# The gate row ahead of the last two experts' scatter, and a later start for GpSimd

## What is computed

```python
for e in range(N_EXPERTS):
    hid = jax.nn.silu(t @ w1[e]) * (t @ w3[e])
    out = out + gate[:, e:e + 1] * (hid @ w2[e])
...
x = x + g_f[:, None] * _hier_moe(hf, ...)
```

## Time and profile before

| | us |
|---|---|
| median of 3 runs | 1541.68 |
| lowest, highest | 1541.16, 1543.71 |
| profiled execution, its own time | 1542.04 |
| its span, first to last instruction | 1540.2 |
| TensorE busy | 1512.9 (98%) |
| VectorE busy | 1186.7 (77%) |
| ScalarE busy | 948.8 (62%) |
| GpSimd busy | 80.1 (5%) |

### The profile page before, as it was taken

The page is one execution under the profiler, slowest core; times in us unless marked ns, Lnnn a source line. Parts: engine busy times, 40 slices in busy tenths (PEclk is TensorE's granted clock), DMA queues, the critical chain, the costliest instruction groups (busy, mean ns, idle before and its releaser), DMA issues.

```text
span 1540.2 us, 20164 instructions
## 1 busy us (share of the span) xinstructions
PE 1512.9 (98%) x7920; PEld 1257.1 (82%) x7920; DVE 1186.7 (77%) x1639; ACT 948.8 (62%) x1503; POOL 80.1 (5%) x78
## 2 busy tenths in 40 slices
PE   9999999999999999999999999999999899999997
PEld 9998888888888799888788887887777778888785
DVE  7568857667888684788576679877667789999998
ACT  6577854755444364878457555544455568888884
POOL 0010000000000000100000000000200000000005
PEclk9999999999999999999999999999999999999999
DMA  7545436437776445453455368884521449999994
GB/s 293 209 142 205 149 137 218 148 127 277 254 269 242 161 177 187 159 191 136 164 191 192 137 244 326 333 321 142 192 103 55 159 188 366 367 380 372 374 365 163
DMA packets 52200, 339.33 MB, mean 220 GB/s; under 512 B 7835, under 2 KB 8477, under 8 KB 13316
## 3 DMA queue, kind: packets, MB, share of 16 engines
q1 hardware_dynamic: 48932, 331.79, 58.3%
q0 software_dynamic: 3168, 6.20, 1.1%
HBM read 332.82 MB, written 10.49 MB: 223 GB/s over the span
## 4 chain that ended last, share of the span: by engine, by line
PE 47%; DVE 6%; ACT 2%; issue 1%; DMA 0%; POOL 0%; DVEq 0%; ACTq 0%
PE bank L842 14%; PE bank L844 13%; PE bank L843 13%; PE bank L848 3%; DVE wls L2285 2%; PE bank L1380 1%; DVE h L2255 1%; ACT whs L1603 1%; PE bank L1362 1%; PE bank L1182 0%; PE bank L1160 0%; DMA raw<-in_ws_dram 0%; PE bank L1099 0%; POOL sm L3256 0%; PE bank L1122 0%
## 5 line engine op out<-in xcount | busy, mean ns | idle before, releaser
L2285 DVE TENSOR_TENSOR wls<-raw,whs 128x1024 fp32r<-128x1024 f32 x432 | 514.1, 1226 | 149.0 <-ACT whs L1603 148.1
L1603 ACT ACTIVATE whs<-raw 128x1024 fp32r<-128x1024 f32 x432 | 435.9, 1052 | 189.1 <-PE bank L844 164.2
L842 PE MATMUL bank<-whs,P1h 128*128 128x512 f32 (+1 forms) x732 | 291.3, 398 | 2.0 <-issue 2.0
L844 PE MATMUL bank<-whs,P1l 128*128 128x512 f32 (+1 forms) x732 | 285.0, 389 | 0.0
L843 PE MATMUL bank<-wls,P1h 128*128 128x512 f32 (+1 forms) x732 | 284.1, 388 | 0.0
L842 PE MATMUL bank<-whs,P0h 128*128 128x512 f32 (+1 forms) x632 | 251.6, 398 | 1.4 <-DVE P0l L2255 1.4
L844 PE MATMUL bank<-whs,P0l 128*128 128x512 f32 (+1 forms) x632 | 245.1, 388 | 0.0
L843 PE MATMUL bank<-wls,P0h 128*128 128x512 f32 (+1 forms) x632 | 244.5, 387 | 0.0
L842 PEld LDWEIGHTS bank<-whs,P1h 128*128 128x128 f32 x732 | 138.0, 188 | 29.9 <-issue 3.4
L844 PEld LDWEIGHTS bank<-whs,P1l 128*128 128x128 f32 x732 | 137.9, 188 | 29.6
L843 PEld LDWEIGHTS bank<-wls,P1h 128*128 128x128 f32 x732 | 138.2, 189 | 26.7
(11 more groups left out here) (298 smaller groups left out, 2521.9 us busy)
## 6 DMA issues: line engine op xcount, KB each, us to landing
raw<-in_ws_dram SPq DMA_DIRECT2D x264, 1024.0 KB, 4.8
landing<-in_ws_dram SPq DMA_DIRECT2D x38, 1024.0 KB, 7.2
lnb<-in_ln_g_dram SPq DMA_DIRECT2D x6, 512.0 KB, 6.1
lnb<-in_ln_b_dram SPq DMA_DIRECT2D x6, 512.0 KB, 7.2
ydram<-arena POOLq DMA_DIRECT2D x4, 512.0 KB, 8.4
mid<-in_bias_dram SPq DMA_DIRECT2D x1, 2048.0 KB, 7.5
h<-in_x_dram SPq DMA_DIRECT2D x2, 512.0 KB, 4.0
lnb<-in_mem_dram SPq DMA_DIRECT2D x1, 1024.0 KB, 12.4
```

The lines of the kernel that those rows point to most:

```text
L842: e.matmul(out, x[0], w[0], start=start, stop=False, skip_group_check=skip)
L844: return e.matmul(out, x[1], w[0], start=False, stop=stop, skip_group_check=skip)
L1603: e.activation(hi, src, ACT.Copy, bias=0.0, scale=1.0).then_inc(*high.done(n, f))
L2285: e.tensor_tensor(lo, src, f32(hi), ALU.subtract).then_inc(*low.done(n, f))
```

## The change

Four things are done, all in the last stage:

- For experts 14 and 15 VectorE multiplies each bank by the gate row into `Y` (new key `yg`), ScalarE copies `Y`, not the bank, to `Yph`, and VectorE subtracts from `Y`, not from the bank. Both products stand ahead of both subtractions. The scatter's result then needs no product, so that VectorE adds the banks to `h` directly, in four additions.
- The order of these additions and of the stores is by column half first, and all four are VectorE's; GpSimd's two last additions are gone.
- GpSimd's product of fetched rows and gate row waits, besides the combination, for the last weight half (`low` of the last unit).
- VectorE's combination for t = 1 (`combined(1)`) moves from chunk 31's `combine` to behind the subtraction of `turn_hidden(31)`. On ScalarE `combine` stays where it is.

```diff
@@ TensorE, down_part and scatter
-                                bank(b, (act if x < NFAR else vec, "ey", x, hf))
+                                bank(b, (act, "ey", x, hf) if x < NFAR else (vec, "yg", x, hf))
...
-                                bank(b, (vec, "fin", t, hf))
+                                bank(b, (vec, "out", t, hf))
@@ ScalarE, down_part
-                        ac.wait_ge(mm, "edn", c, hf)
-                        wait_for(start)
                         if x < NFAR:
+                            ac.wait_ge(mm, "edn", c, hf)
+                            wait_for(start)
...
                         else:
+                            ac.wait_ge(vec, "yg", x, hf)
                             if x > NFAR:
                                 ac.wait_ge(mm, "eacc", x - 1, 1, 1)
-                            put(Yp[0][:, o], banks[b][:, :], ACT.Copy, "ey", x, hf)
+                            put(Yp[0][:, o], Y[x % 2][:, o], ACT.Copy, "ey", x, hf)
@@ VectorE, turn_hidden
                     tt(hid[1][:, s_], halves(banks[7][:, 0:256]), f32(hid[0][:, s_]), ALU.subtract, "ehT", c)
+                    if c == 2 * NEXP - 1:
+                        combined(1)
@@ VectorE, down_part
                     for hf in range(2):
                         b = ((6, 4) if x == NEXP - 1 else (3, 6) if x % 2 else (2, 1))[hf]
                         o = slice(hf * 512, (hf + 1) * 512)
+                        ve.wait_ge(mm, "edn", c, hf)
+                        ve.wait_ge(sent[x % 2], x - 2)
+                        ve.wait_ge(vec, "rows", 3)
+                        tt(Y[x % 2][:, o], banks[b][:, :], gab[:, 1, o], ALU.mult, "yg", x, hf)
+                    for hf in range(2):
+                        o = slice(hf * 512, (hf + 1) * 512)
                         ve.wait_ge(act, "ey", x, hf)
-                        tt(Yp[1][:, o], banks[b][:, :], f32(Yp[0][:, o]), ALU.subtract, "ey", x, hf)
+                        tt(Yp[1][:, o], Y[x % 2][:, o], f32(Yp[0][:, o]), ALU.subtract, "ey", x, hf)
@@ VectorE, combine
                 def combine(t):
+                    if t == 0:
+                        combined(t)
+
+                def combined(t):
                     a, b = far[t], far[2 + t]
@@ VectorE, the end
-                for t in range(2):
-                    for n in range(2):
-                        s_, o = slice(n * 512, (n + 1) * 512), arr(512 * (2 * n + t), 512)
+                for n in range(2):
+                    for t in range(2):
+                        s_ = slice(n * 512, (n + 1) * 512)
                         ve.wait_ge(mm, "eacc", NEXP - 1, t, n)
-                        tt(o, banks[2 * n + t][:, :], gab[:, 1, s_], ALU.mult, "fin", t, n)
-                        if n:
-                            ve.wait_ge(vec, "fin", t, n)
-                            ve.wait_ge(pool, "h", t)
-                            tt(h[:, t, s_], h[:, t, s_], o, ALU.add, "out", t, n)
+                        ve.wait_ge(pool, "h", t)
+                        tt(h[:, t, s_], h[:, t, s_], banks[2 * n + t][:, :], ALU.add, "out", t, n)
@@ GpSimd
                     po.wait_ge(vec, "comb", t)
+                    po.wait_ge(low, len(plan) - 1, 1)
                     po.wait_ge(vec, "rows", 3)
...
-                for t in range(2):
-                    po.wait_ge(vec, "fin", t, 0)
-                    po.wait_ge(pool, "h", t)
-                    e.tensor_tensor(h[:, t, 0:512], h[:, t, 0:512], arr(512 * t, 512), ALU.add).then_inc(*pool.done("out", t, 0))
@@ SyncE, stores
-            def stores(key):
-                for t in range(2):
-                    for n in range(2):
-                        sp.wait_ge((pool, vec)[n], key, t, n)
+            def stores(key, by):
+                for n in range(2):
+                    for t in range(2):
+                        sp.wait_ge(by[n], key, t, n)
...
-                stores("out")
+                stores("out", (vec, vec))
```

More of the change, by code:

```diff
@@ L3436, in sparse @@
                 weights(list(paths[1]))
-                stores("out")
+                stores("out", (vec, vec))
             def dense():
                 weights(list(paths[0]))
-                stores("dout")
+                stores("dout", (pool, vec))
             two_ways(sp, None, sparse, dense)
```

## The result

| | before | changed |
|---|---|---|
| median of 14 runs, us | 1540.93 | 1543.88 |
| lowest, highest | 1539.91, 1544.25 | 1542.51, 1545.60 |
| profiled execution: time, span | 1542.04, 1540.2 | 1544.08, 1542.3 |
| VectorE's end, from z | 16.06 | 17.37 |
| end of the span, from z | 19.70 | 22.77 |

The ratio of the changed kernel's time to the one before is 1.0017, 95% interval 1.0010 to 1.0025: the changed kernel is slower, by 2.95 us between the medians. The forecast was 1542.1 with a range up to 1543.3, so the time lies above the range.

The account below looks back on a forecast made before the run. VectorE rows held behind GpSimd's instructions were taken to delay down chunk 31. The 1.4 us gained there was eaten by GpSimd's late sum, leaving plus 0.43 on the median 1541.68: 1542.1 us, range 1540.2 to 1543.3.

Parts of the forecast that it names:

- The waiting and its release: Ahead of down chunk 31: P0l waits for whole GpSimd instructions; holding GpSimd back cuts a weight half to 1.23 us.
- The gain on TensorE at down chunk 31: Down chunk 31 on TensorE starts at 1525.79 instead of 1527.17, a gain of 1.4 us.
- The stall ahead of chunk 30: TensorE waits about 0.2 us for Pall of chunk 30, behind the gate products and copies of expert 14.
- The combination for t = 1: On VectorE behind Pall of chunk 31: asked at 1524.9, waits for GpSimd's first product, runs 1526.01 to 1527.15.
- The step that failed: Expert 15's first subtraction on VectorE is asked 0.11 us ahead of GpSimd's product for t = 1 and goes first.
- rival G: GpSimd's product for t = 1 goes ahead of expert 15's first subtraction: plus 1.1, 1542.8, or 1543.1 at worst; chance 0.27.
- the stores: At the end: span ends 3.64 us behind the last addition as before; three close stores cost at most 1.09 us.
- The high end: Upper end of the range: rival G's worse form plus 0.3 for the noise of a median, given as 1543.3.
- the idle stretch of over 1 us between the first and second final addition: Sign on VectorE: after the first final addition it idles over 1 us, until GpSimd's sum ends.
- Rival F: Expert 15's short subtractions meet no whole-instruction lock or slip between GpSimd's instructions: 1.2 us less, 1540.5; chance 0.22.
- Rival H: The stall ahead of chunk 30 is longer, shifting everything 1 us for 1: 1543.1 at 1 us; chance 0.08.
- Same: Whole kernel: a measurement, which tells about 0.2% (3.1 us), would not part it from no change; chance 0.94.

Follow-up runs that it names:

- e9: Changed kernel with 14 and 6 filling matmuls on TensorE, ahead of the scatter of expert 15 and between its halves; +2.90 us against before.
- e10: The changed kernel itself, run again without any edit; +2.87 us against before.
- e7: The kernel before, with all four stores waiting for the last addition; +2.57 us against before.
- e12: The kernel before with all four stores behind its last addition, a repeat of e7; +2.38 us against before.
- e13: The changed kernel with all four stores behind its last addition; +4.21 us against before.
- e8: Changed kernel with 28 and 14 filling matmuls on TensorE, ahead of the scatter of expert 15 and between its halves; +4.49 us against before.
- e4: Changed kernel, but for expert 15 the first subtraction stands ahead of the second gate product; +1.20 us against before.
- e3: Changed kernel, but the gate product is written back into its bank, and copy and subtraction read the bank; +0.59 us against before.
- e14: e3 with additions and stores by half of the tokens, VectorE making the t = 1 sum, all stores behind the last addition; +1.06 us against before.
- e1: The changed kernel without GpSimd's wait for the last weight half; +2.44 us against before.

## Why the prediction was wrong

The forecast was 0.4 us over before, and 2.95 came. Of the 2.5 us between them, 0.9 lie at VectorE's end (+1.31 instead of +0.43) and 1.6 behind it.

- **The waiting and its release were right.** Long `P0l` rows come from waiting behind whole GpSimd instructions, and GpSimd's wait removes that: 1.21 and 1.22 us measured, 1.23 predicted. The gain on TensorE at down chunk 31 was put at 1.4 and is 1.38. The stall ahead of chunk 30 was put at 0.2 and is 0.13 (0.36 in place of 0.23 from z). The combination for t = 1 was to end 1.1 behind GpSimd's product and ends 1.07 behind it (1526.17, 1525.10).
- **The step that failed: "First subtraction: asked at 1529.39, runs 1529.42 to 1529.97. GpSimd product t = 1: asked at 1529.50".** The 0.08 us between GpSimd's sum and its next product were taken from a product and the sum that depends on it. The product for t = 1 depends on nothing in the sum ahead of it and starts 0.04 us before the sum's recorded end (1528.38 against 1528.42). The subtraction therefore comes second, not first, in both profiled executions of the changed kernel. This is rival G, which I gave 0.27. The request of the subtraction was put at z + 8.89 and came at 8.90; with the right gap the product's would have been at 8.88, and G the forecast by 0.01 us. With so small a margin either order could have been forecast.
- **A term that was missing: TensorE's clock.** G's price was plus 1.1 at VectorE's end; 1.31 came. TensorE stands idle for 3.54 us in that case, the granted clock is 0.50 behind it, and e9 prices this at 0.43 us. Without the half clock 0.88 would have come, so G's price was 0.2 too high and its closeness to 1.31 is in part luck.
- **The term that was mis-sized most: the stores.** The sum took "3.64 behind the addition" over from before, and bounded three stores close together at no more than 1.09. In the profiled execution it was 5.40, in its repetition e10 5.50, and the medians put 1.6 us more than before behind VectorE's end. e7 and e12 show that a bunch of stores costs 2.4 to 2.6 us with VectorE's end unchanged, and in the changed kernel the stores do come closer: before, GpSimd's long chain let them go in two pairs, and now all four additions, and so all four stores, come behind the second subtraction. That this closeness makes the 1.6 us is argued and not shown (see e13, e8 and e9). Counted from before, this term alone carried the time out of the range: the range reached up to +1.6, and without it +1.3 would have come.
- **The ends of the range.** It was added to 1541.68, the median of three runs; fourteen gave 1540.93, 0.75 less, which made the miss look smaller than it is. The high end adds up to 1543.4 and not 1543.3.
- A sign that did not come: the idle stretch of over 1 us between the first and second final addition. It belongs to a first addition that is done before GpSimd's sum, as in e4 (1.73 idle) and e3 (2.71). In the changed kernel the second subtraction waits for that sum, and the additions follow it without a gap.
- Rival F (subtractions slip between) had 0.22 and was wrong: six of six subtractions of 128x512 with both operands in SBUF, asked for while GpSimd ran (changed kernel, e4 and e10), waited, and the two of e3 with one operand in a bank did not. Rival H's stall did not grow.
- "Same" had 0.94, with 0.2% as what a measurement can tell. The measured 0.17% lies under that, but its interval (1.0010 to 1.0025) excludes no change: it is a small loss and not "the same".

**What stays open.** Why an issue of SyncE takes 1.3 to 1.8 us in some kernels and 0.35 in others. It was 1.38 in the changed kernel, 1.29 in e10, 1.53 in e9, but never over 0.44 in e4, whose last three stores were also 0.6 us apart. A long issue is not the loss itself: e4 has none, and its span ends 5.0 us behind the start of its last issue. And what sets the end behind the last issue, 3.1 us in e14 to 5.3 in e10. The kernel before with its stores by column half, or the changed one with its stores by tokens and nothing else, would test the order of the quarters; neither was run.

## What to carry to other kernels

Before a scheduler's gain is booked, list every instruction with two SBUF operands that lies beside GpSimd work, and play out who asks first. Where the second operand can stay in a PSUM bank, leave it there: e3 changes nothing else and takes 1.7 us off VectorE's end. When a wait is moved off one engine, ask what now comes behind the engine that was delayed: here VectorE's second subtraction waits for GpSimd's last sum, and four additions and four stores queue behind it. And don't take the stores' part over from the old kernel when their order or spacing changes: e7 and e12 moved nothing but the stores and lost 2.4 to 2.6 us.

## What the runs showed of the hardware

- In these rows an instruction that waited for the other engine ends a nearly fixed time behind it: 0.55 us for 128x512 and 1.07 to 1.09 for 128x1024 on VectorE, 2.22 to 2.27 for 128x1024 on GpSimd (2.22: the first subtraction ended at 1531.27, the sum at 1530.80 + 2.69 = 1533.49).
- GpSimd's product for t = 1, which doesn't depend on the sum ahead of it, started 0.04 us before that sum's recorded end (1528.38 against 1528.42); a sum that needs the product ahead of it started 0.08 us behind its end (1521.14 against 1521.06).
- VectorE can multiply a bank by an SBUF row in place, 0.70 us for 128x512 against 0.69 into SBUF.
- TensorE stood at half clock (0.50) in the scatter of 15 after idle stretches of 3.54 us (changed kernel) and 3.51 (e1). It was 1.00 after 1.26 and 1.58 (e4) and 1.38 (e3).
- A filling matmul of 128x128 in plain float32 shows as two records and takes 0.22 us of TensorE's time: 28 of them, 56 records, stood for 6.17 us between the start of the first and that of the scatter (e8).
- Four stores in a bunch behind the last addition instead of in two pairs: +2.57 us (e7) and +2.38 (e12), with VectorE's end at z + 15.98 and 16.01 (before 16.06).
